# The tiles fh and fl of the second and third feed-forward block moved to the first block's place

## What is computed

```python
def swiglu(h, w_gate, w_up, w_down):
    return (jax.nn.silu(h @ w_gate) * (h @ w_up)) @ w_down

# first block
hn = rms_norm(h, norm2_g)
gate, up = jnp.split(hn @ w_gate_up, 2, axis=-1)
return h + (jax.nn.silu(gate) * up) @ w_down
# second block, before and after its attention
x = x + 0.5 * swiglu(rms_norm_2(x, ffn1_norm[i]), ffn1_w_gate[i], ffn1_w_up[i], ffn1_w_down[i])
x = x + 0.5 * swiglu(rms_norm_2(x, ffn2_norm[i]), ffn2_w_gate[i], ffn2_w_up[i], ffn2_w_down[i])
```

## The kernel before

| tile | column in the arena | bytes into a 256-byte line |
|---|---|---|
| fh, fl of block 0 | 0 and 11264 | 128 |
| fh, fl of block 1 | 32 and 11296 | 0 |
| fh, fl of block 2 | 48 and 11312 | 64 |
| tmp | 22592 | 128 |
| mh, ml, m2h, m2l, ath, atl, yfh, ysh and others that matmuls of 512 columns read | | 128 |
| xh, xl, outside the arena, from token column 16 on, where such matmuls read them | | 128 |
| sk2, keys of the last attention, read on line 947: even heads, odd heads | | 128, 64 |

## Time and profile before

### The profile page before, as it was taken

How to read it: one execution, slowest core, us unless ns; L and a number is a source line. 1 busy time by engine, 2 the same in 40 slices (tenths; PEclk the granted TensorE clock), 3 DMA queues, 4 the chain that set the end, 5 groups by cost and what they waited for, 6 DMA issues and landing times.

```text
span 2095.4 us, 26593 instructions
## 1 busy us (share of the span) xinstructions
PE 2053.9 (98%) x9561; PEld 1671.5 (80%) x9561; DVE 884.6 (42%) x1394; ACT 754.2 (36%) x1038; POOL 999.5 (48%) x753
## 2 busy tenths in 40 slices
PE   8999999999999999999999999998899999999999
PEld 7798886688888888888888887886578888888877
DVE  6788735534333321343333124565653533331114
ACT  6412224434222223322222234666654332222232
POOL 5345442145555554455554445554434455554443
PEclk9999999999999999999999999999999999999999
DMA  4232331113333323333332232111113333332232
GB/s 156 71 96 81 101 100 61 41 60 100 101 100 100 92 88 107 95 96 88 97 100 91 95 96 81 61 50 52 41 61 101 100 99 88 94 100 95 91 105 81
DMA packets 250057, 184.01 MB, mean 88 GB/s; under 512 B 7040, under 2 KB 247168, under 8 KB 249984
## 3 DMA queue, kind: packets, MB, share of 16 engines
q1 hardware_dynamic: 249296, 182.74, 29.0%
q10 hardware_dynamic: 688, 0.31, 0.1%
HBM read 180.93 MB, written 2.10 MB: 87 GB/s over the span
## 4 chain that ended last, share of the span: by engine, by line
PE 89%; DVE 4%; ACT 2%; POOL 2%; issue 1%; DMA 0%; SPq 0%; DVEq 0%; ACTq 0%; POOLq 0%
PE ps L545 27%; PE ps L547 27%; PE ps L546 27%; POOL wlo L454 2%; DVE sc L1435 1%; PE ps L766 1%; PE ps L751 1%; PE ps L832 1%; PE ps L834 1%; PE ps L833 1%; DVE pu L1936 1%; PE ps L909 1%; DVE ssum L1563 0%; PE ps L765 0%; ACT whi L1305 0%
## 5 line engine op out<-in xcount | busy, mean ns | idle before, releaser
L454 POOL TENSOR_TENSOR wlo<-raw,whi 128x512 fp32r<-128x512 f32 (+1 forms) x692 | 938.2, 1386 | 978.3 <-ACT whi L1005 924.7
L545 PE MATMUL ps<-xh,whi 128*128 128x512 f32 (+2 forms) x1912 | 736.6, 385 | 12.9 <-DVE xl L1435 7.4
L547 PE MATMUL ps<-xh,wlo 128*128 128x512 f32 (+2 forms) x1912 | 723.2, 378 | 0.0
L546 PE MATMUL ps<-xl,whi 128*128 128x512 f32 (+2 forms) x1912 | 722.8, 378 | 0.0
L1005 ACT ACTIVATE whi<-raw 128x2048 fp32r<-128x2048 f32 (+1 forms) x159 | 297.5, 1871 | 802.3 <-PE ps L547 799.8
L545 PEld LDWEIGHTS ps<-xh,whi 128*128 128x128 f32 (+1 forms) x1912 | 359.4, 188 | 82.9 <-issue 11.7
L547 PEld LDWEIGHTS ps<-xh,wlo 128*128 128x128 f32 (+1 forms) x1912 | 358.6, 188 | 68.4
L546 PEld LDWEIGHTS ps<-xl,whi 128*128 128x128 f32 (+1 forms) x1912 | 359.4, 188 | 64.5 <-issue 2.5
L1489 DVE TENSOR_TENSOR tmp<-ps,rs 128x512 f32<-128x512 f32 x148 | 102.1, 692 | 325.8 <-PE ps L547 308.6
L545 PE MATMUL ps<-fh,whi 128*128 128x512 f32 x528 | 207.3, 393 | 0.0
L546 PE MATMUL ps<-fl,whi 128*128 128x512 f32 x528 | 207.3, 393 | 0.0
(11 more groups left out here) (296 smaller groups left out, 2178.3 us busy)
## 6 DMA issues: line engine op xcount, KB each, us to landing
raw<-in_w_in SPq DMA_DIRECT2D x90, 512.0 KB, 4.6
raw<-in_w_gate_up SPq DMA_DIRECT2D x44, 512.0 KB, 4.7
raw<-in_ffn_w_gate SPq DMA_DIRECT2D x44, 512.0 KB, 4.0
raw<-in_ffn_w_up SPq DMA_DIRECT2D x44, 512.0 KB, 5.2
raw<-in_ffn_w_down SPq DMA_DIRECT2D x32, 512.0 KB, 4.3
raw<-in_w_down SPq DMA_DIRECT2D x16, 512.0 KB, 4.0
raw<-in_ffn_w_down SPq DMA_DIRECT2D x16, 384.0 KB, 3.4
raw<-in_w_b SPq DMA_DIRECT2D x8, 512.0 KB, 4.1
```

The costliest lines, as they stand in the source:

```text
L454: ins = pool.tensor_tensor(wlo[:, c % 2, cs], raw[:, c % 2, cs], whi[:, c % 2, cs].bitcast(F32), ALU.subtract)
L545: pe.matmul(o, w_of(whi), xhi, start=first, stop=False)
L546: pe.matmul(o, w_of(whi), xlo, start=False, stop=False)
L547: return pe.matmul(o, w_of(wlo), xhi, start=False, stop=last)
```

## The change

The tiles fh and fl of blocks 1 and 2 are put where those of block 0 stand, 128 bytes into a 256-byte line: there is one fh and one fl now, at columns 0 and 11264. tmp moves from column 22592 to 22528, right behind fl, 256 bytes further down and as before 128 bytes into a line. The pad ahead of the arena is written in another way and has the same 16 columns as before, so the arena and all else stay where they were. On each engine the instructions and their order are the same as before, and so are all waits; only the addresses in those that use fh, fl and tmp differ. After the change the lines 51 to 143 have numbers smaller by 1, and those from 145 on greater by 1.

```diff
-F_AT = (0, 32, 48)
...
         arena_cols = 27648
-        pad = sb("pad", [P, (128 - (nc.sbuf_base + 31) // 32 * 32) % 256 // 4 or 64])
+        lead = (128 - (nc.sbuf_base + 31) // 32 * 32) % 256 // 4
+        if lead:
+            sb("pad", [P, lead])
         start = (nc.sbuf_base + 31) // 32 * 32
         arena = sb("arena", [P, arena_cols])
...
-        fh = [at(f"fh{f}", o, [P, FK, T], F32R) for f, o in enumerate(F_AT)]
-        fl = [at(f"fl{f}", FK * T + o, [P, FK, T], F32R) for f, o in enumerate(F_AT)]
-        tmp = at("tmp", 2 * FK * T + 64, [P, 4, T])
+        fh = at("fh", 0, [P, FK, T], F32R)
+        fl = at("fl", FK * T, [P, FK, T], F32R)
+        tmp = at("tmp", 2 * FK * T, [P, 4, T])
...
                                     mm = passes(ps[:, bank(c + j, t), :], cr % 2, lambda wt: wt[:, cr % 2, o:o + P],
-                                                fh[f][:, k0 + k, :], fl[f][:, k0 + k, :], r == 0 and k == 0, r == 2 and k == kn - 1)
+                                                fh[:, k0 + k, :], fl[:, k0 + k, :], r == 0 and k == 0, r == 2 and k == kn - 1)
...
-                    act.activation(one(fh[f], lin(n, per, i)), tmp[:, 3, :], ACT.Copy).then_inc(h_hi, 1)
+                    act.activation(one(fh, lin(n, per, i)), tmp[:, 3, :], ACT.Copy).then_inc(h_hi, 1)
...
-                        dve.tensor_tensor(one(fl[f], nn), tmp[:, 3, :], one(fh[f], nn).bitcast(F32), ALU.subtract).then_inc(h_split, 1)
+                        dve.tensor_tensor(one(fl, nn), tmp[:, 3, :], one(fh, nn).bitcast(F32), ALU.subtract).then_inc(h_split, 1)
```

## The result

The kernel takes 2090.15 us (median of 7 runs, 2089.48 to 2091.32) where the kernel before took 2097.22 us beside it (7 runs, 2095.87 to 2097.32): 7.07 us less, a ratio of 0.9968 with a 95% interval of 0.9957 to 0.9980. The forecast was 2089.35 us, in a range of 2087.3 to 2092.0: the result is faster, by the size that was forecast.

A forecast was written before the change was run, and what follows sets the result against it. TensorE, busy 2053.9 of 2095.4 us, was taken as the bound; 3.46 + 3.47 = 6.93 us off two blocks' stretches, all other terms 0, took the 2096.28 us median to 2089.35 us, range 2087.3 to 2092.0.

The forecast's parts named there:

- The bound and the three stretches: TensorE bounds the kernel, busy throughout each block's 528 matmuls reading fh and fl: 119.73, 123.19 and 123.20 us.
- Items 1 and 2: fh and fl of second and third block moved to 128 bytes: their stretches drop to 119.73 us, saving 3.46 and 3.47 us.
- the close place behind GpSimd: First block's stretch: GpSimd's four adds end at 795.18 us, TensorE starts on their result at 795.45, a margin of 0.27 us.
- What is different about them: Section on the three blocks: same code, but fh and fl start 128, 0 and 64 bytes into a line, setting the pace.
- The three observations: Evidence for place: xh and xl at 128 take 389 to 390 ns, mh at 128 389, odd heads' sk2 at 64 394.
- Item 3: Stages before and after the stretches keep their operands, places and pace; their waits move with the stretch's end.
- Item 4: VectorE's adds writing fl (line 1517): 44 might grow by 15 to 18 ns, 0.7 us in sum, but hidden; taken as 0.
- The 0.7 us that widened the range: Allowance either way in the range, for VectorE and ScalarE operations if they come onto the path.
- Items 5 to 7: tmp 256 bytes further down, the pad unchanged, no wait added or removed: 0 each, tmp's bounded by 0.7 us either way.
- What is late next: Whether weights come too late for faster TensorE: second block's margin behind GpSimd's adds falls from 1.65 to 1.34 us, gain kept.
- The rival in which TensorE outruns its weights: Weight preparation exceeds the 1.34 us margin left, costing at six places in the two stretches: 2101.1 us, chance 1%.
- The rule of 16-byte lines: Counter-rule from the Trainium skill: all three places are multiples of 16 bytes, so alike; sum 0, 2096.3 us.

The follow-up runs named there:

- e9: Kernel before with only the second block's fh and fl moved to 128 bytes, the third's left at 64: 2092.54 us against 2096.72, ratio 0.9983.
- e5: Kernel after with data and weights, all but hT and vec, shifted together by 64 bytes: 2088.83 us against 2096.72 for the kernel before, ratio 0.9962.
- e4: Kernel before with whi and wlo shifted 64 bytes to 192; fh and fl at 128, 192, 0 in blocks 0, 1, 2: 2128.29 us against 2096.34.
- e1: Kernel before with places exchanged, fh and fl at 64 bytes in block 0, 128 in blocks 1 and 2: 2092.93 us against 2096.34, ratio 0.9983.
- e3: Kernel before with fh and fl at 32 and 96 bytes in blocks 0 and 1, 128 one line further in block 2: 2095.75 us against 2096.34.

## Why the prediction was right, point by point

**The bound and the three stretches** held as read: TensorE without a gap, 528 matmuls, and one matmul's length as the only thing that differs.

**Items 1 and 2.** 3.46 + 3.47 = 6.93 us were forecast and 3.52 + 3.52 = 7.04 measured in the stretches, 7.07 in the medians. The stretches came out 0.05 us shorter than the 119.73 us that stood as their price. In that first block's stretch, before and after, the starts slip by 0.03 to 0.05 us between the 180th and the 190th matmul, at the close place behind GpSimd. But in e9 and e5 the first block has as little margin there (0.27 and 0.28 us) and no slip (119.68 us in both), so why it slips stays open. The median itself came out 0.8 us above the forecast, because the kernel before was 0.94 us slower in its seven runs (2097.22) than in the three that the forecast started from (2096.28).

**The reason was wrong in part.** The section "What is different about them" took the place in the line, 128 bytes, for the cause. For this change it is the same thing, since the weights stand at 128 bytes too; but e4 and e5 show that it is the distance to the weights. The three observations couldn't tell the two apart: in each of them the weights stand at 128. The first one (xh is fast right behind the third block's stretch) did rule out the time; the source of the weights, which isn't the same in the two stages, was ruled out by e1 only. Looking at where all operands of the slow instruction stand, the weights too, would have named the second reading before any run; it would not have moved the forecast.

**Item 3** held: 241.13 us between the first two stretches, 241.12 before; and from the third block's first add on line 1518 to its stretch 223.5 us, as before. Of line 948 (947 before) two heads were read in the kernel after, 394 ns for an odd one and 389 for an even one, as forecast.

**Item 4** asked whether the adds that write fl get slower at the first block's place. They don't. In the kernel after, all three blocks use the same tiles (line 1517 is 1518 there):

```profile
L1518 DVE TENSOR_TENSOR fl<-tmp,fh x22: 775/784/786, 533.2 to 761.6; 128x512 f32 x22
...
L1518 DVE TENSOR_TENSOR fl<-tmp,fh x22: 743/761/779, 899.1 to 1122.5; 128x512 f32 x22
...
L1518 DVE TENSOR_TENSOR fl<-tmp,fh x22: 744/768/775, 1685.9 to 1914.3; 128x512 f32 x22
```

784, 761 and 768 ns against 784, 766 and 769 in the earlier trace rows: there it is the block, not the place, that differs. The 0.7 us that widened the range were not there; what makes the first block's adds longer was not tried. **Items 5 to 7** left no trace in the stretches: TensorE is busy for the whole of each, with nothing lost beyond the forecast.

**What is late next.** In the second block GpSimd's four adds and TensorE's start on their result:

```profile
1151.96 5.03 POOL L455 TENSOR_TENSOR wlo<-raw,whi 128x512 fp32r<-128x512 f32 x4 [5.43 <-ACT whi L1006]
...
1158.34 0.39 PE L546 MATMUL ps<-fh,whi 128*128 128x512 f32 x1
```

They end at 1156.99, and TensorE starts at 1158.34: 1.35 us of margin, where 1.34 were worked out from the earlier trace rows. The rival in which TensorE outruns its weights had no footing.

**The rule of 16-byte lines.** The Trainium skill, "SBUF — State Buffer", section "Specifications (TRN2)", gives lines of 16 bytes, with a cost for crossing to a new one. By these alone all distances in the table, which are multiples of 16, would be alike; the measurement, from 119.7 to 123.7 us, decides against that. The Trainium skill also says, in "SBUF — State Buffer", section "Who interferes with whom", that TensorE has two read ports, one for the moving operand and one for the weight loads, which are independent. Here they are not independent in what they cost: in e4 only the weights moved under xl and mh, and these matmuls became 5 ns longer. Where the two meet, no run shows.

**The lucky part.** The number was right with the wrong cause in hand, because the weights happen to stand at 128 bytes like the first block's tiles: moving the others there set the distance to 0. The sum leaned on less than that: its price was the measured pace of the block whose addresses were taken over, whatever made that block fast.

## What to carry to other kernels

Where TensorE is the bound and float32r matmuls of 512 columns follow each other with a weight load each, put the moving operands and the weights at the same place within their 256-byte lines: here most mismatches cost 16 clock cycles in 544 (119.7 against 123.2 us for 528 matmuls, at 2.4 GHz), and shifting the weights against nearly all data (e4) cost 32 us in 2096. Compare the same instruction, of the same shape, from one stretch to the next; a difference of 5 ns in the means of hundreds of records has a cause and is worth looking for. And when an address seems to matter, list those of all operands, and shift one against the other before naming a good address.

## What the runs showed that I had not expected

- The pace depends on the distance between the moving operand and the weights, whose loads overlap the matmuls in the records, with a sharp optimum at 0. Two distances that differ by 256 bytes gave the same time both times that this was tried (0 in e3, 64 in e4). 64 bytes cost a third of what most others do, and -64 the whole: it isn't symmetric.
- The cost comes in steps. At the full clock, 2.4 GHz, three matmuls take 1,632 cycles at distance 0 (119.68 us / 176 x 2.4), 1,648 at 64 and 1,680 at most other distances: 16 and 48 more.
- Matmuls of 256 columns (chunks in which the weights are the moving operand, lines 832 to 834) were faster at another distance, in the one run that changed it. In e4, where it went from 0 to 64, their records are 4 ns shorter than in the kernel after (the line with the low part of x, in the kernel after and in e4):

```profile
L835 PE MATMUL ps<-whi,xl 128*128 128x256 f32 x128 | 36.2, 283 | 0.0
```

```profile
L836 PE MATMUL ps<-whi,xl 128*128 128x256 f32 x128 | 35.7, 279 | 0.0
```

With 384 of them (three lines of 128) this is worth 1 us or so in this kernel, an estimate from 4 ns a record; no version for it was built, and other distances were not tried for them.
